# Rescaling by the norm moved behind the matmuls in the first four prenorms of a two-part transformer block

## What is computed

```python
def rmsnorm(x, g):   # the prenorm and the postnorm
    y = xf * lax.rsqrt(jnp.mean(xf * xf, axis=-1, keepdims=True) + EPS)
    return (y * g.astype(jnp.float32)).astype(x.dtype)

f = swiglu(rmsnorm(h, ffn1_pre_g[l]), ...)      # silu(h @ w_gate) * (h @ w_up) @ w_down
h = h + 0.5 * rmsnorm(f, ffn1_post_g[l])
m = hybrid_mixer(rmsnorm(h, mix_pre_g[l]), w_in[l], ...)
h = h + rmsnorm(m, mix_post_g[l])
f = swiglu(rmsnorm(h, ffn2_pre_g[l]), ...)
h = h + 0.5 * rmsnorm(f, ffn2_post_g[l])
```

## Time and profile before

| | us |
|---|---|
| median of three runs | 2926.79 |
| the profiled execution | 2924.85 |
| its span | 2923.1 |
| TensorE busy | 2713.2 (93%) |
| VectorE busy | 1242.1 (42%) |
| GpSimd busy | 1078.6 (37%) |
| ScalarE busy | 914.7 (31%) |

### The profile page before, as it was taken

How to read it: one execution, slowest core, us unless ns; L and a number is a source line. 1 busy time by engine, 2 the same in 40 slices (tenths; PEclk the granted TensorE clock), 3 DMA queues, 4 the chain that set the end, 5 groups by cost and what they waited for, 6 DMA issues and landing times.

```text
span 2923.1 us, 34995 instructions
## 1 busy us (share of the span) xinstructions
PE 2713.2 (93%) x13196; PEld 2148.3 (73%) x13196; DVE 1242.1 (42%) x1440; ACT 914.7 (31%) x1351; POOL 1078.6 (37%) x539
## 2 busy tenths in 40 slices
PE   6999988998899879999889779999998869999999
PEld 5999987733676758888658348888876547888887
DVE  3111231124644661212355455766135674666412
ACT  3222123354233332221243423222234353222223
POOL 4443444212122344444444134444433203444443
PEclk9999999987899989999999979999999979999999
DMA  3222331101111213223212012222322101323322
GB/s 140 91 88 78 85 96 58 32 0 38 44 51 51 72 53 99 93 90 90 94 61 94 0 53 98 93 100 94 101 87 87 58 1 65 101 93 98 103 94 72
DMA packets 65649, 219.16 MB, mean 75 GB/s; under 512 B 8401, under 2 KB 8529, under 8 KB 65554
## 3 DMA queue, kind: packets, MB, share of 16 engines
q1 hardware_dynamic: 63792, 216.42, 23.0%
q10 hardware_dynamic: 1762, 1.45, 0.2%
HBM read 215.74 MB, written 2.10 MB: 75 GB/s over the span
## 4 chain that ended last, share of the span: by engine, by line
PE 85%; DVE 9%; ACT 2%; issue 2%; POOL 1%; DMA 0%; SPq 0%; DVEq 0%; ACTq 0%; PEldq 0%; PEld 0%; POOLq 0%
PE PS L289 25%; PE PS L290 25%; PE PS L291 25%; PE PS L1084 1%; PE PS L1113 1%; PE PS L1100 1%; DVE ntmp L490 1%; PE PS L1098 1%; PE PS L1499 1%; PE PS L2367 1%; DVE h L609 1%; PE PS L1476 1%; DVE asx L2411 1%; DVE ast__141 L2413 1%; DVE asx L2432 1%
## 5 line engine op out<-in xcount | busy, mean ns | idle before, releaser
L284 POOL TENSOR_TENSOR wlo<-wraw,whi 128x1024 fp32r<-128x1024 f32 (+2 forms) x425 | 989.0, 2329 | 1536.7 <-ACT whi L277 1536.7
L289 PE MATMUL PS<-xh,whi 128*128 128x512 f32 (+2 forms) x2544 | 911.3, 358 | 37.2 <-DVE xl L461 22.1
L290 PE MATMUL PS<-xl,whi 128*128 128x512 f32 (+2 forms) x2544 | 897.2, 353 | 0.0
L291 PE MATMUL PS<-xh,wlo 128*128 128x512 f32 (+2 forms) x2544 | 896.7, 352 | 0.0
L277 ACT ACTIVATE whi<-wraw 128x1024 fp32r<-128x1024 f32 (+2 forms) x425 | 429.0, 1010 | 1043.2 <-PE PS L291 1039.4
L289 PEld LDWEIGHTS PS<-xh,whi 128*128 128x128 f32 (+1 forms) x2544 | 478.3, 188 | 121.2 <-issue 35.6
L291 PEld LDWEIGHTS PS<-xh,wlo 128*128 128x128 f32 (+1 forms) x2544 | 479.4, 188 | 66.8 <-issue 0.9
L290 PEld LDWEIGHTS PS<-xl,whi 128*128 128x128 f32 (+1 forms) x2544 | 479.4, 188 | 59.7 <-issue 0.5
L289 PE MATMUL PS<-hid2h,whi 128*128 128x512 f32 x560 | 217.8, 389 | 0.0
L290 PE MATMUL PS<-hid2l,whi 128*128 128x512 f32 x560 | 217.8, 389 | 0.0
L291 PE MATMUL PS<-hid2h,wlo 128*128 128x512 f32 x560 | 217.8, 389 | 0.0
(11 more groups left out here) (413 smaller groups left out, 3415.4 us busy)
## 6 DMA issues: line engine op xcount, KB each, us to landing
wraw<-w_up_dram SPq DMA_DIRECT2D x96, 512.0 KB, 3.3
wraw<-w_dn_dram SPq DMA_DIRECT2D x48, 512.0 KB, 3.3
wraw<-w_f1gu_dram SPq DMA_DIRECT2D x44, 512.0 KB, 3.3
wraw<-w_f2gu_dram SPq DMA_DIRECT2D x44, 512.0 KB, 3.3
wraw<-w_hyin_dram SPq DMA_DIRECT2D x24, 512.0 KB, 3.3
wraw<-w_win_dram SPq DMA_DIRECT2D x18, 512.0 KB, 3.2
wraw<-w_gate_dram SPq DMA_DIRECT2D x16, 512.0 KB, 3.4
wraw<-w_pg_dram SPq DMA_DIRECT2D x16, 512.0 KB, 3.3
```

The costliest lines, as they stand in the source:

```text
L284: pool.tensor_tensor(wlo[:, s, 0:size], wraw[:, s, 0:size], whi[:, s, 0:size].bitcast(F32), ALU.subtract).then_inc(lo_done.s, 1)
L289: pe.matmul(out_, whi[:, s, a:b], xhi, start=start, stop=False, skip_group_check=True)
L290: pe.matmul(out_, whi[:, s, a:b], xlo, start=False, stop=False, skip_group_check=True)
L291: return pe.matmul(out_, wlo[:, s, a:b], xhi, start=False, stop=stop, skip_group_check=True)
```

## The change

`s_prenorm` and `s_postnorm` go. The four projections behind them get x times gain, unscaled, and multiply by the factor `rbx` after the matmul: on VectorE in `s_gate_up` (both the gate before Silu and the product) and `s_win`, and in `s_hyin` on VectorE into a buffer `zh`, from which ScalarE evacuates as before. The new `s_post_raw` adds the normalised output to `h` and, per tile, makes the high part (ScalarE), the low part (VectorE), the square (ScalarE) and the running sum (VectorE); the factor comes from `root`, which TensorE reaches only behind the first chunks. There is no barrier from `s_out` to the next projection. The first group of chunks (four; in `s_hyin` the gates' chunk and three) runs with the contraction outermost for six of the eight tiles (`OUTER`), in banks of its own, and is then finished chunk by chunk. `s_out` squares on ScalarE straight from PSUM. The factor 0.5 is a bias of Exp. The gates' 8 columns stand in one chunk of 36 columns, rows 0 to 3 and 32 to 35 of one bank. At the start SyncE issues x tiles 0 and 1, `vec`, chunk 0 of the weights, x tiles 2 to 7, chunks 1 and 2, `con`, chunk 3.

The core of the diff (indentation cut by eight; of rewritten functions only the new lines):

```diff
+    summed, scaled_high, scaled_low, squared, added = raw_tile("n1", "ffn1_pre", (xh, xl), TK, landed=True)
     def sp(sp):
+        load_x(sp, (0, 1))
...
     def act(act):
         act.preload_act_table_set("natural_log_exp_and_others")
+        act.wait_ge(*vec_landed(16))
+        scaled_high(act, 0)
+        scaled_high(act, 1)
+        split_hi(act, 0, 0)
+        for t in range(2, DT):
+            scaled_high(act, t)
+        split_hi(act, 0, 1)
         for t in range(DT):
+            squared(act, t)
+            if t in (2, 5):
+                split_hi(act, 0, 2 + t // 4)
     def dve(dve):
+        dve.wait_ge(*vec_landed(16))
         for t in range(DT):
...
+            scaled_low(dve, t)
...
+def also_load(sp, k):
+    if k == 0:
+        load_x(sp, range(2, DT))
+    if k == 2:
+        sp.dma_start(con[:, :], d["con"]).then_inc(con_landed.s, 16)
...
+            dve.tensor_tensor(acc[:, 0:n], acc[:, 0:n], sq[:, 0:n], ALU.add).then_inc(summed.s, 1)
+    if landed:
+        return summed, scaled_high, scaled_low, squared, added
+    return kept, summed, scaled_high, scaled_low, squared, squared_here, added
+def root(summed, rb, n=T, bank_=6):
     total, ln_done, rb_done = local("root", total=1, ln=1, rb=1)
+    H = 2 if n == TK else 1
+    w = n // H
     def pe(pe):
         pe.wait_ge(*summed(DT))
+        for i in range(H):
+            ins = pe.matmul(PS3[:, bank_ + i, 0:w], c_("ones"), acc[:, i * w:(i + 1) * w], start=True, stop=True,
+                            skip_group_check=True)
+        ins.then_inc(total.s, 1)
     def act(act):
         act.preload_act_table_set("natural_log_exp_and_others")
         act.wait_ge(*total(1))
+        act.activation(rb[:, 0:n].rearrange("p (a q) -> p a q", a=H), bank(bank_, H, w), ACT.Ln, bias=epsc[:, 0:1],
+                       scale=1.0 / D).then_inc(ln_done.s, 1)
         act.wait_ge(*ln_done(1))
+        act.activation(rb[:, 0:n], rb[:, 0:n], ACT.Exp, scale=-0.5).then_inc(rb_done.s, 1)
     return pe, act, rb_done
...
+def s_post_raw(gain, n, factor, f, parts, tag, next_gain):
...
     def pe(pe):
+        pe.wait_ge(*most_summed)
+        for i in range(H):
+            pe.matmul(PS3[:, 6 + i, 0:w], c_("ones"), acc[:, i * w:(i + 1) * w], start=True, stop=False,
+                      skip_group_check=True)
+        pe.wait_ge(*last_squared)
+        for i in range(H):
+            ins = pe.matmul(PS3[:, 6 + i, 0:w], c_("ones"), sq[:, i * w:(i + 1) * w], start=False, stop=True,
+                            skip_group_check=True)
+        ins.then_inc(total.s, 1)
...
+    def act(act):
+        act.wait_ge(*total(1))
+        act.activation(lnv[:, 0:n].rearrange("p (a q) -> p a q", a=H), bank(6, H, w), ACT.Ln,
+                       bias=epsc[:, 0:1], scale=1.0 / D).then_inc(ln_done.s, 1)
+        act.wait_ge(*ln_done(1))
+        act.activation(rbc[:, 0:n], lnv[:, 0:n], ACT.Exp, bias=epsc[:, 2:3] if factor == 0.5 else 0.0,
+                       scale=-0.5).then_inc(rbc_done.s, 1)
         for t in range(DT):
...
+            scaled_high(act, t)
+            squared(act, t)
+    def dve(dve):
+        def scale(t):
             if t >= 2:
...
+                dve.wait_ge(*kept(t - 1))
             dve.scalar_tensor_tensor(scaled_f[:, t % 2, 0:n], f[:, t, 0:n], v_(gain, t), rbc[:, 0:n],
                                      ALU.mult, ALU.mult).then_inc(scaled.s, 1)
...
+        def add(t):
+            dve.wait_ge(*scaled(t + 1))
+            dve.tensor_tensor(h[:, t, 0:n], scaled_f[:, t % 2, 0:n], h[:, t, 0:n], ALU.add).then_inc(kept.s, 1)
+        dve.wait_ge(*rbc_done(1))
+        scale(0)
+        add(0)
+        for t in range(DT):
+            if t + 1 < DT:
+                scale(t + 1)
+            scaled_low(dve, t)
+            if t + 1 < DT:
+                add(t + 1)
+            if t >= 1:
+                added(dve, t - 1)
+        added(dve, DT - 1)
+    stage(pe, act, dve)
...
+def spread(rb, H):
+    a = rb[:, :]
+    if H == 2:
+        return bass.AP(tensor=a.tensor, offset=a.offset, ap=[a.ap[0], [0, 2], [TK // 2, 2], [1, TK // 2]])
+    return bass.AP(tensor=a.tensor, offset=a.offset, ap=[a.ap[0], [0, 2], [1, T]])
...
+def s_gate_up(name, xn, n, summed):
...
+    g_read, u_free, g_act, whole, hid_hi, hid_lo = local(
...
+        if H == 2:
+            for k in range(4):
+                if k == 3:
+                    pe.wait_ge(*con_landed(16))
+                    pe_root(pe)
+                    pe.wait_ge(*rb_done(1))
+                chunk(0, k, k == 0)
+            with pe.Fori(1, turns) as j:
+                turn(j)
+            return
+        for kt in range(OUTER):
+            xn_ready(pe, xn, kt)
+            for k in range(4):
+                s, _, g = slot_of(base, k, 4, 0)
+                if kt == 0:
+                    pe.wait_ge(*lo_done(g + 1))
+                tile(pe, k, s, kt, 4)
+        for k in range(4):
+            s, _, g = slot_of(base, k, 4, 0)
+            for kt in range(OUTER, DT):
+                if k == 0:
+                    xn_ready(pe, xn, kt)
+                ins = tile(pe, k, s, kt, 4)
+            ins.then_inc(chunk_used.s, 1)
+        for k in range(4):
+            if k == 3:
+                pe.wait_ge(*rb_done(1))
+            chunk(1, k)
+            if k == 0:
+                pe_root(pe)
+        with pe.Fori(2, turns) as j:
+            turn(j)
+    def high(act, j):
+        act.wait_ge(*whole(j + 1))
+        act.activation(dh[:, bass.ds(2 * H * j, 2 * H), :], pra[:, :, :], ACT.Copy).then_inc(hid_hi.s, 1)
+    def opened(act, j):
+        act.wait_ge(*g_read(j + 2))
+        act.activation(sga[:, :, :], sga[:, :, :], ACT.Silu).then_inc(g_act.s, 1)
...
+        def turn_act(j, ahead):
+            high(act, j - 1)
+            ahead(0)
+            ahead(1)
+            opened(act, j)
+            ahead(2)
+            ahead(3)
...
+        def turn(j, b0, first):
+            dve.wait_ge(*chunk_used(base + 2 + 4 * j))
+            dve.wait_ge(*u_free(j + 1))
+            dve.tensor_tensor(pair(sga[:, :, :]), pair(bank(b0, 2 * H, w)), spread(rbx, H),
+                              ALU.mult).then_inc(g_read.s, 1)
+            if not first:
+                low(dve, j - 1)
             dve.wait_ge(*chunk_used(base + 4 + 4 * j))
+            dve.wait_ge(*g_act(j + 1))
+            dve.wait_ge(*hid_lo(j + 1))
+            dve.tensor_tensor(pra[:, :, :], sga[:, :, :], bank(b0 + 2 * H, 2 * H, w), ALU.mult).then_inc(u_free.s, 1)
             dve.wait_ge(*u_free(j + 2))
+            dve.tensor_tensor(pair(pra[:, :, :]), pair(pra[:, :, :]), spread(rbx, H), ALU.mult).then_inc(whole.s, 1)
...
+def s_out(name, kts, rhs, n, tiles_per_turn, led, f):
...
+        def square(t):
+            act.wait_ge(*chunk_used(base + nl * (t + 1)))
+            if t >= 2:
+                act.wait_ge(*summed(t - 1))
+            act.activation(split((acc if t == 0 else sq)[:, 0:n]), bank(H * (t % 2), H, w),
+                           ACT.Square).then_inc(sqd.s, 1)
+        for t in range(DT):
+            for c in range(nl):
+                if c == nl - 1:
+                    square(t)
+                split_hi(act, base, t * nl + c + 4)
...
+        for t in range(DT):
+            dve.wait_ge(*sqd(t + 1))
+            dve.tensor_scalar(split(f[:, t, 0:n]), bank(H * (t % 2), H, w), 1.0, None, ALU.mult).then_inc(free.s, 1)
+            if 1 <= t < DT - 1:
+                if t >= 2:
+                    dve.wait_ge(*summed(t - 1))
+                dve.tensor_tensor(acc[:, 0:n], acc[:, 0:n], sq[:, 0:n], ALU.add).then_inc(summed.s, 1)
...
+def s_win(summed):
...
+    def first_bank(c):
+        return c if c < 4 else (4, 0, 2)[(c - 4) % 3]
...
+                q_tile(c, kt)
+        for c in range(4):
+            for kt in range(OUTER, DT):
+                if c == 0:
+                    xn_ready(pe, "n2", kt)
+                ins = q_tile(c, kt)
+            ins.then_inc(chunk_used.s, 1)
+        pe_root(pe)
+        for c in range(4, count):
+            s, _, g = slot_of(base, c)
+            if c >= 5:
+                pe.wait_ge(*read({5: 2, 6: 4}[c] if c < 7 else c - 2))
+            pe.wait_ge(*lo_done(g + 1))
+            for i in range(2):
+                for kt in range(DT):
+                    ins = mm3(pe, PS3[:, first_bank(c) + i, 0:W], s, kt * P, (kt + 1) * P,
+                              xh[:, kt, i * W:(i + 1) * W], xl[:, kt, i * W:(i + 1) * W], kt == 0, kt == DT - 1)
+            ins.then_inc(chunk_used.s, 1)
+            if 9 <= c < 13:
+                turn_v(pe, c - 9)
...
     def dve(dve):
+        dve.wait_ge(*rb_done(1))
+        def take(c):
+            dve.wait_ge(*chunk_used(base + c + 1))
+            b = first_bank(c)
+            if c < 4:
...
+                dst = ks[:, c - 4, :] if c < 8 else vtmp[:, c % 2, :] if c < 12 else ckv[:, c - 12, :]
+                ins = dve.tensor_tensor(halves(dst, TK), bank(b, 2, W), halves(rbx[:, :], TK), ALU.mult)
```

(88 more changed lines are left out.)

580 lines of the change are left out of this document (218 added, 362 removed).

## The result

The changed kernel takes 2848.51 us (median of 4 runs, 2844.78 to 2849.72), the kernel before, in the same series, 2925.37 (4 runs, 2922.73 to 2927.04): a ratio of 0.9743, with a 95% interval of 0.973 to 0.9756. The prediction was 2857.3, with 2843 to 2877 as its range. The profiled execution took 2847.57.

What follows compares the result with a forecast made beforehand. TensorE bounds the kernel (85% of the chain), losing some 136 us at four junctions. Savings 17.5 + 17.5 + 20.8 + 13.7 = 69.5 took 2924.85 to 2855.4, plus 1.9 to the median: 2857.3 us, range 2843 to 2877.

Steps and rivals of the forecast that it cites:

- The start: Kernel start, up to chunk 3: 14.5 to 18.2 us lost instead of 34.6; taken as -17.5 us.
- First junction: `f1dn` to `s_win`: 12.7 us lost instead of 34.6, less new waits at copies; -17.5 us.
- ring: Post norm: add, high, square, added through VectorE and ScalarE in program order set tile arrivals 3.3 us apart.
- The waits at the copies: `s_win`, `s_hyin`: `keep` queued behind take or scale makes TensorE wait three times, 1.7 and 1.5 us each; +5.1, +4.5.
- Second junction: Into `s_gate_up` (f2gu): 12.4 us lost instead of 33.2; -20.8 us.
- Third junction: Into `s_hyin`: chunk 3 over at 41.1 us instead of 61.0, less copy waits and smaller costs; -13.7 us.
- The scan: `s_hyin`: gates' scan between scale(3) and scale(4) brings scaled(5) close to when chunk 7 wants its bank; +1 us.
- The loops: Gate-up turns have one more hop, all under 22 us of matmuls per turn; no cost.
- rival E: Head of a `s_gate_up` turn: ScalarE's waits delay weight splits, 4 us in each of 20 turns; 2937 us; chance 0.03.
- Rival D: Junction chain: GpSimd's splits beside it slow the lows, 1.2 us more in each of 15 rounds; 2875 us; chance 0.15.
- Rival C: Clock stays at half through tile arrivals, 15 us more at each of three junctions; 2902 us; chance 0.07.
- Rival B: Copies' waits do not show and arrivals keep TensorE's own 2.7 us pace; 2840 us; chance 0.13.

Runs made afterwards that it cites:

- e6_load_order: Changed kernel with the load order undone: all eight x tiles, `vec` and `con` ahead of the weights; 2854.7 us.
- e1_keep_first: Changed kernel with the copy of transposed values, `keep`, ahead of the next chunk's take or scale in `s_win` and `s_hyin`; 2840.35 us.
- e4_fourth_bank: Changed kernel with chunk 3 of `s_hyin` writing the unused bank 1, so it needs no evacuation and no root; 2844.53 us.
- e3_contract_inner: Changed kernel with `OUTER` 0, chunk by chunk in `s_gate_up`, `s_win` and `s_hyin`; 2894.81 us.
- e2: Changed kernel with ScalarE making the next tile's high half before it squares this one, in the raw post norm; 2840.45 us.

## Why the prediction was right, and where not

**The start, -17.5: measured -17.6**. First matmul at 11.07 (near 10 forecast), half rate to 15.2, a wait of 1.4 for the eighth low, 1.5 for the root as forecast; chunk 3 is over at 40.5 (37.8 to 41.5). GpSimd's splits hold up VectorE's lows, two of which took 2.33 and 2.87 instead of 0.76, so that the last was ready at 17.0, just behind the 14 to 16.7 that I gave; the splits themselves took 2.35 and 2.40, so the other half of my sentence, that the lows hold up the splits, hardly shows. The load order was in this forecast, but without a price of its own: it is 5.9 us (e6_load_order).

**First junction, -17.5: -17.6.** Sums 2.06 (2.15 forecast), Exp done at 3.55 (3.6), first tile 7.1 (7.1), ring 3.35 (3.3), eighth low done 28.2 (28.5), all 96 over 33.2 (34.0). The contention on the first scale was 0.36 (0.5 taken). The waits at the copies were 1.7, three times, as priced. That the sum is off by only 0.1 is partly luck: the 96 matmuls were over 0.8 earlier than forecast, and the rest of the stage took 0.7 more. Of that, some 0.4 are the copies, which cost 5.5 by e1_keep_first for 5.1, and some 0.3 the end of the stage, where TensorE's wait at the barrier shrank from 1.3 to 0.9 and not by the 0.7 that I took.

**Second junction, -20.8: -21.6.** The last three lows start 3.27 apart. The eighth was done at 27.6 us (28.5 forecast), mostly because the third tile was ready at 11.3 and not at 12.0: it came 2.15 behind the second, as the second behind the first, where I had 2.7. That is the 0.8. The root stands between chunks as forecast.

**Third junction, -13.7: -14.5.** 96 matmuls over at 32.5 (33.4), for the same reason, chunk 3 at 38.7 (39.3) behind a wait of 5.2 (4.8). The copies' waits 1.5 each, as priced (4.8 us in all by e1_keep_first, for 4.5). The scan cost 0 where I had 1 (bounds 0 and 5): the gap of 5.2 gave it slack, and it comes up as a wait of 1.6 as soon as that gap is closed (e4_fourth_bank).

**The loops, 0: held.** From 45 to 403 and from 1056 to 1385 us TensorE waits for nothing; rival E had no ground. Rival D did not come either: the lows at the junctions took 0.75 to 0.77 us, not 2.

**The clock.** Rival C, the half clock through the arrivals, did not come: 0.99 from 414.3 on, with TensorE busy 20.94 of 22.7 us. It is real one step away, though: with one chunk instead of four per tile (e3_contract_inner) TensorE is busy 12.09 of 22 us, even at half rate, and stays there. And in `s_stick`, whose matmuls are small (128 to 512 columns, many over 16 or 64 rows), the clock of the changed kernel goes back and forth (windows, as above):

```profile
545.00:554.00 9.00, 9.00 (x23) 2.64 (x22) 3.35 (x7) 4.42 (x12) 1.72 (x3) 1.00 0.00 0
555.00:561.00 6.00, 6.00 (x12) 2.05 (x11) 3.10 (x8) 2.70 (x7) 1.68 (x3) 0.50 0.00 0
562.00:571.00 9.00, 9.00 (x23) 2.64 (x22) 2.67 (x6) 4.43 (x12) 1.40 (x4) 1.00 0.00 0
572.00:578.00 6.00, 6.00 (x11) 1.94 (x11) 2.05 (x6) 2.79 (x7) 1.21 (x3) 0.50 0.01 3
```

The rule of the Trainium skill that I weighed (TensorE: Matmul & The Clock Gate, on a second HAM failure mode, short idles between groups of matmuls) does not describe the junction. It does not describe this stretch either: the clock does go back and forth, but the rows have TensorE busy for 9.00 of 9.00 and 6.00 of 6.00 us, with no idle between groups. The kernel before does the same there (clock 0.54 from 571 to 578.5 us, 1.00 from 578.5 to 588.5, TensorE busy throughout). I weighed the rule for the edited stages alone and did not ask what a clock that goes back and forth does to the rest.

**The step that failed** is the one that stands nowhere in the sum: that untouched stages take the same time. They gave 5.9 us, and the sum of the forecast terms was 1.8 short: together the 7.7 by which the profiled execution (2847.57) beat its forecast of 2855.4, but for rounding. Rival B, more gain through a tighter ring and free copies, was wrong as a forecast and right as a plan: both need an edit (e1 and e2), and give 10.3 and 5.5 instead of its 9.6 and 7.5.

## What to carry to other kernels

When operands arrive one by one, give each arrival all the work that can use it: the loop order brought 42 of 54 us at the three junctions, since it turns waiting into work and keeps the clock up. When a step is moved onto another engine's in-order queue, look at what that engine did just before: a copy queued behind work that waits for TensorE itself costs TensorE the wait, and swapping two lines gives it back. And compare stages, not totals: an edited stage repeated within 0.6 us where the five runs of one kernel lay 5 to 18 us apart.
